# Modulation weights as 64 rows by two column blocks over the partitions: one sum over partitions per vector instead of two

## The reference, cut to what matters

```python
c_silu = jax.nn.silu(c)
mods = jnp.split(c_silu @ ada_w[layer] + ada_b[layer], N_MOD, axis=-1)   # N_MOD = 9, each vector 1024 wide
shift, scale = jnp.split(c_silu @ kv_ada_w + kv_ada_b, 2, axis=-1)
h = modulate(rms_norm(x, norm_g[layer, 0]), sh, sc)                      # h * (1 + sc) + sh
```

## Time and profile before

| what | us |
|---|---|
| median of 3 runs | 1204.28 |
| the runs | 1204.13 to 1204.91 |
| the profiled execution, its own time | 1204.4 |
| span of the profiled execution, first to last instruction | 1202.0 |
| PE busy in it | 1186.9 |
| DVE busy | 799.3 |
| ACT, POOL busy | 586.4, 559.0 |
| DMA, mean | 248 GB/s, 297.92 MB |

### The profile page before, as it was taken

How to read it: one execution, slowest core, us unless ns; L and a number is a source line. 1 busy time by engine, 2 the same in 40 slices (tenths; PEclk the granted TensorE clock), 3 DMA queues, 4 the chain that set the end, 5 groups by cost and what they waited for, 6 DMA issues and landing times.

```text
span 1202.0 us, 15430 instructions
## 1 busy us (share of the span) xinstructions
PE 1186.9 (99%) x5752; PEld 976.4 (81%) x5752; DVE 799.3 (66%) x1118; ACT 586.4 (49%) x764; POOL 559.0 (47%) x417
## 2 busy tenths in 40 slices
PE   9999999999999999999999999999999999999998
PEld 6888788788788888788888888888888887888887
DVE  6885468845786787678768666697673675644423
ACT  5566555665643443454434357444352665544440
POOL 1465334565454443545444226664452463445360
PEclk9999999999999999999999999999999999999999
DMA  9976369845798899459888748798874444766650
GB/s 352 361 272 230 106 237 336 282 161 171 240 349 293 288 352 346 158 169 340 297 309 307 275 176 283 243 332 300 305 296 166 149 156 158 262 218 203 210 192 35
DMA packets 183224, 297.92 MB, mean 248 GB/s; under 512 B 8368, under 2 KB 100208, under 8 KB 183152
## 3 DMA queue, kind: packets, MB, share of 16 engines
q1 hardware_dynamic: 177696, 284.82, 68.0%
q10 hardware_dynamic: 5456, 12.13, 2.9%
HBM read 295.84 MB, written 1.08 MB: 247 GB/s over the span
## 4 chain that ended last, share of the span: by engine, by line
PE 88%; DVE 5%; ACT 2%; issue 1%; SPq 1%; DMA 1%; POOL 1%; ACTq 0%; DVEq 0%
PE ps L1831 26%; PE ps L1844 26%; PE ps L1836 26%; PE ps L2097 2%; PE ps L1981 1%; PE ps L1923 1%; PE ps L1858 1%; PE ps L2009 1%; DVE w_lo L1164 1%; PE ps L1997 1%; DMA raw<-w_in 1%; POOL stat L507 1%; PE ps L1969 1%; PE ps L2020 1%; SPq L474 1%
## 5 line engine op out<-in xcount | busy, mean ns | idle before, releaser
L516 POOL TENSOR_TENSOR w_lo<-raw,w_hi 128x512 fp32r<-128x512 f32 x348 | 480.2, 1411 | 442.5 <-ACT w_hi L647 442.5
L647 ACT ACTIVATE w_hi<-raw 128x2048 fp32r<-128x2048 f32 x188 | 354.5, 1910 | 104.0 <-PE ps L1844 69.3
L1831 PE MATMUL ps<-w_hi,h_hi 128*128 128x512 f32 x1120 | 314.0, 402 | 1.1 <-issue 0.8
L1844 PE MATMUL ps<-w_lo,h_hi 128*128 128x512 f32 x1120 | 301.7, 391 | 1.8 <-DVE w_lo L1164 1.4
L1836 PE MATMUL ps<-w_hi,h_lo 128*128 128x512 f32 x1120 | 300.7, 391 | 0.0
L1164 DVE TENSOR_TENSOR w_lo<-raw,w_hi 128x2048 fp32r<-128x2048 f32 x96 | 223.7, 2334 | 110.8 <-ACT w_hi L647 108.7
L1844 PEld LDWEIGHTS ps<-w_lo,h_hi 128*128 128x128 f32 x1120 | 209.5, 188 | 49.3 <-DVE w_lo L1164 4.0
L1836 PEld LDWEIGHTS ps<-w_hi,h_lo 128*128 128x128 f32 x1120 | 210.4, 188 | 45.9 <-DVE h_lo L1225 0.2
L1831 PEld LDWEIGHTS ps<-w_hi,h_hi 128*128 128x128 f32 x1120 | 200.9, 189 | 43.7 <-issue 6.8
L1150 DVE SCALAR_TENSOR_TENSOR ps<-ada_raw,ccol,ps 128x512 f32<-128x512 f32 x240 | 181.1, 754 | 8.8 <-DMA ada_raw<-ada_w 2.0
L920 ACT ACTIVATE a_hi<-ps 128x512 fp32r<-128x512 f32 x44 | 26.4, 599 | 159.8 <-PE ps L2097 159.8
(11 more groups left out here) (198 smaller groups left out, 978.6 us busy)
## 6 DMA issues: line engine op xcount, KB each, us to landing
raw<-ffn_in SPq DMA_DIRECT2D x176, 512.0 KB, 5.7
ada_raw<-ada_w SPq DMA_DIRECT2D x144, 512.0 KB, 7.2
raw<-ffn_out SPq DMA_DIRECT2D x44, 1024.0 KB, 6.6
raw<-w_in SPq DMA_DIRECT2D x31, 1024.0 KB, 8.8
raw<-w_out SPq DMA_DIRECT2D x8, 1024.0 KB, 5.7
ada_raw<-kv_ada_w SPq DMA_DIRECT2D x16, 512.0 KB, 8.6
raw<-w_kv SPq DMA_DIRECT2D x8, 1024.0 KB, 5.6
bias<-na_bias ACTq DMA_DIRECT2D x16, 256.0 KB, 4.5
```

The lines of the kernel that those rows point to most:

```text
L516: ins = pool.tensor_tensor(w_lo[:, u % RAW, piece], raw[:, u % RAW, piece], w_hi[:, u % RING, piece].bitcast(F32), ALU.subtract)
L647: act.activation(w_hi[:, u % RING, :], raw[:, u % RAW, :], ACT.Copy).then_inc(*S.inc("w_hi_ready", u))
L1831: pe.matmul(bank(b), hi[:, k_in_lhs + k, tok], wh[:, k, c * 512:(c + 1) * 512], start=start and k == 0, stop=False)
L1844: ins = pe.matmul(bank(b), hi[:, k_in_lhs + k, tok], wl[:, k, c * 512:(c + 1) * 512], start=False, stop=stop and k == nk - 1)
```

## The change

The slots hold another cut of the same weights. The partitions are now two blocks of 64: partition p of block k holds a weight row of half k of the columns. A slot is 2 x 64 rows by both halves (1024 columns), so a vector takes 8 slots in one chain of 16 multiply-adds, and one set of four transposes and one reduction for all of it. The layout of silu(c) (`ccol`, 16 columns of 64 rows, twice over the partitions) follows. A slot is now loaded by two DMAs, one for each 64 partitions. `ada_after` is the same table of 160 slots.

```diff
 ADA_RING = 4
+ADA_BLOCKS = 2
-SUM_STEPS = (5, 7, 9, 11, 12, 14, 15, 18, 22, 31)
+SUM_STEPS = (5, 7, 9, 11, 12, 14, 15, 18, 31)
-    HALF_SLOTS = KC // 2
-    N_ADA = N_VEC * 2 * HALF_SLOTS
+    ADA_ROWS, ADA_SET = P // ADA_BLOCKS, ADA_BLOCKS // 2
+    SLOTS, N_SETS = D // (2 * ADA_ROWS), N_VEC // ADA_SET
+    N_ADA = N_SETS * SLOTS
...
-                    rows = w[2 * pair * P:(2 * pair + 2) * P, col:col + 512].rearrange("(k p) n -> p k n", p=P)
-                    sp.dma_start(ada_raw[:, j % ADA_RING], rows).then_inc(ada_in[j % ADA_RING], 16)
+                    for k in range(ADA_BLOCKS):
+                        w, col = vec_src[ADA_SET * g + k // 2]
+                        col += 512 * (k % 2)
+                        rows = w[2 * slot * ADA_ROWS:(2 * slot + 2) * ADA_ROWS, col:col + 512]
+                        sp.dma_start(ada_raw[k * ADA_ROWS:(k + 1) * ADA_ROWS, j % ADA_RING],
+                                     rows.rearrange("(i p) n -> p i n", p=ADA_ROWS)).then_inc(ada_in[j % ADA_RING], 16)
...
-            def reduce_vector(v, half):
-                dve.wait_ge(*S.at("ada_sumT_done", v, half))
-                b = job_bank["ada", v, half]
-                dve.tensor_reduce(mods[:, v, 4 * half:4 * half + 4], bank(b).rearrange("p (k c) -> p k c", k=4),
-                                  AX.X, ALU.add).then_inc(*S.inc("ada_reduced", v, half))
-                if half == 0:
-                    return
+            def reduce_set(g):
+                dve.wait_ge(*S.at("ada_sumT_done", g))
+                blocks = bank(job_bank["ada", g]).rearrange("p (k b r) -> p b k r", k=4, b=ADA_BLOCKS)
+                vectors = range(ADA_SET * g, ADA_SET * g + ADA_SET)
+                m = mods[:, ADA_SET * g:ADA_SET * g + ADA_SET, :].rearrange("p v (h k) -> p (v h) k", h=2)
+                dve.tensor_reduce(m, blocks, AX.X, ALU.add).then_inc(*S.inc("ada_reduced", g))
...
-                for half in sum_step.get((layer, 31), []):
-                    reduce_vector(*half)
+                lows(o + 3)
+                for g in sum_step.get((layer, 31), []):
+                    reduce_set(g)
                 fill(o + 3)
...
-            def ada_sum(v, half):
-
-                pe.wait_ge(*S.at("ada_used", (2 * v + half) * HALF_SLOTS + HALF_SLOTS - 1))
-                b = job("ada", (v, half), ("ada_reduced", v, half))
+            def ada_sum(g):
+
+                pe.wait_ge(*S.at("ada_used", g * SLOTS + SLOTS - 1))
+                b = job("ada", (g,), ("ada_reduced", g))
...
-        "c_cols": cols(get("c_2")[0]),
+        "c_cols": np.tile(get("c_2")[0].reshape(-1, P // ADA_BLOCKS).T, (ADA_BLOCKS, 1)),
```

More of the change, by code:

```diff
@@ L235, in program @@
             taken.add((layer, s))
-            sum_step[layer, s] = [(v, half)]
+            sum_step[layer, s] = [g]
             continue
@@ L240, in program @@
                 e = first[b] + wait + (wait > 1 and first[b] + wait in sum_unit.values())
-        sum_unit[v, half] = e
-    in_pool = max(h for h in sum_unit if sum_unit[h] < first["pool"])
+        sum_unit[g] = e
+    in_pool = max(g for g in sum_unit if sum_unit[g] < first["pool"])
     sum_unit[in_pool] = first["pool"]
-    for h in range(2, len(HALVES)):
-        if HALVES[h - 2] in sum_unit:
-            assert sum_unit[HALVES[h - 2]] + 2 < half_end(*HALVES[h]), HALVES[h]
+    for g in range(2, N_SETS):
+        if g - 2 in sum_unit:
+            assert sum_unit[g - 2] + 2 < set_loaded(g), g
     def up_sum(e):
@@ L255, in up_sum @@
         return None
-    vec_end = [sum_unit.get((v, 1), 0) + 4 for v in range(N_VEC)]
+    vec_end = [sum_unit.get(v // ADA_SET, 0) + 4 for v in range(N_VEC)]
     with ExitStack() as ctx:
@@ L399, in short_work @@
         def short_work(layer, s):
-            work = [("ada_reduce", half) for half in sum_step.get((layer, s - 1), [])]
+            work = [("ada_reduce", g) for g in sum_step.get((layer, s - 1), [])]
             work += [("diff", h) for h in range(HEADS_DA) if DA_DIFF[h] == s]
@@ L410, in short_work @@
             work += [("da_scores", h) for h in range(HEADS_DA) if DA_SCORES[h] == s]
-            work += [("ada", half) for half in sum_step.get((layer, s), [])]
+            work += [("ada", g) for g in sum_step.get((layer, s), [])]
             return work
@@ L1182, in sums @@
                     u = sums_done[0]
-                    for v, half in HALVES:
-                        e = sum_unit.get((v, half), NU)
+                    for g in range(N_SETS):
+                        e = sum_unit.get(g, NU)
                         if e + 4 == u and up_sum(e) is None and e != first["pool"]:
-                            reduce_vector(v, half)
+                            reduce_set(g)
                     for j in ada_at(u):
@@ L1526, in reduce_sums @@
                 def reduce_sums(s):
-                    for v, half in HALVES:
-                        if up_sum(sum_unit.get((v, half), NU)) == (name, s):
-                            reduce_vector(v, half)
+                    for g in range(N_SETS):
+                        if up_sum(sum_unit.get(g, NU)) == (name, s):
+                            reduce_set(g)
                 for s in range(4 * NG):
```

66 lines of the change are left out of this document (34 added, 32 removed).

## The result

The changed kernel takes 1325.47 us at the median against 1204.28: ratio 1.1002, 95% interval 1.0987 to 1.1017. Of its four runs one, 1349.06, ran in a slower state; the median of the other three is 1325.25. I had forecast 1194.0 in a range to 1204. The forecast was wrong in its sign, and the time lies far above rival 1 as well (1228).

A forecast was written before the change was run, and what follows sets the result against it. PE, busy 1186.9 of 1202.0 us, was taken as the bound; 9.2 us (sums) plus 1.5 (w_lo) off, slower loads costing nothing, gave 1193.6, stated as 1194, with a range from 1191.5 to 1204.

The forecast's parts named there:

- rival 1: Slot loads: half-height loads take the full double (f = 2), both FFN stages lose 17 us, 1228 us; chance 0.13 for slower.
- f: Factor on the slots' load time from half-height loads: taken between 1.2 and 1.5, costing nothing below 1.63 in first FFN.
- my sum: Whole run: 9.2 + 1.5 = 10.7 us off the profiled span, 1202.0 to 1191.3, so 1193.6 expected of the runs.
- 21 us of free queue: Window 320 to 465: loads take 124 us of 145 by bytes over rates, leaving 21 us to absorb slower slots.
- The cover: Tightest place, ffn_out raw loads: w_lo ready 8.8 us ahead of PE; with the queue's free time, 30 us of cover.
- Sums: 20 sets of four transposes leave PE between half steps, 0.46 us each: 9.2 us gained, low bound 7.0.
- w_lo: Ends of both encoder layers: two w_lo made ahead of the reduction gain 1.04 and 0.35 to 0.5, 1.5 us in all.
- In the pooling stage the reduction: Pooling stage: bias and finish now follow the reduction, some 0.4 us, hidden by DVE's 0.78 us idle for ACT.
- the reduction, bias and finish now come behind, about 1.1 us: Encoder layers' ends: these follow w_lo while DVE waits for PE's product; costs nothing, by 0.4 us of cover.
- DVE, the reduction's form: DVE: summing eight rows of 64 instead of four of 128 takes 0.69 us, at worst twice that, off the path.
- SP: SP issues 160 DMAs more, 0.47 us each, 75 us within its 766 us of waiting for PE: costs nothing.
- the signs of rival 1: Slots landing well over 10 us, FFN DMA share near 1 at fewer GB/s, PE waiting for weights in the ffn_out product.

The follow-up runs named there:

- split_rows: Kernel before with each slot's load issued as two of 256 KB, each to all 128 partitions, cut by columns; 1203.9 us, ratio 1.000.
- interleaved: Changed kernel with the two blocks on alternate partitions (row r of block k on partition 2r + k, not 64k + r); 1199.81 us, ratio 0.9964.
- Interleaved_gap: The kernel interleaved plus an unused tile of 32 bytes per partition behind ccol; 1193.14 us, ratio 0.9907.

## Why the prediction was wrong, point by point

- **Loads, the step that failed.** "I take a factor f between 1.2 and 1.5, since the two halves of many slots are queued together ..., so that one can write one half while another writes the other." No row stood behind that sentence. It was an argument, and it served to set aside the one source that had measured such a load. As my sum uses it (all that the queue loses, put down to the slots' bytes, with the other loads as fast as before) f came out at 2.1 to 2.25. Two things are in that number. A slot's own packets take 1.59 times as long, just over my range and near the 1.67 that I had worked out by the Trainium skill ("SBUF — State Buffer", the section on the port swizzle) from two single transfers of 1 MiB; on the slots' own packets the trace agrees with that page. The rest is the slowing of the loads beside them, 99 of the 263 us, a term that stood in no sum of mine, with either f.
- **The price of a given f, the second failure.** Rival 1 had f = 2 and came to 1228. Its 21 us of free queue came from bytes over rates, with SP's queue alone. The engines' share in that window is 0.93, ACT's queue included, which leaves 10 us:

```profile
320.00:465.00 145.00, 145.00 (x679) 119.57 (x679) 115.44 (x137) 62.18 (x52) 69.30 (x50) 1.00 0.93 328
```

With 10 in place of 21 my own formula, 47.4 (f - 1) less 19, gives 33 to 41 us a stage for f of 2.1 to 2.25. The first FFN lost 41 and the second 35. And I priced these two stages only: the encoder lost 25 (PE is busy 17.60 of 20 us from 60 on already) and the third FFN 17. Half the slots cut showed that a mean factor of 1.55, which I had called free, costs 51 us in all. In the very rows that I showed, the share is 1.03 for 30 us: there nothing was free, whatever the mean over the stage.
- **The cover.** I priced only raw loads, with ACT's lead of 8.8 us. That DVE waits for slots in program order, ahead of the gates, stood in no step, though the diff shows the wait and the trace of before the 2.0 us. It is the larger way to PE (45.8 us at L2105).
- **The clock** was no term of mine: some 35 of the 123.5 us, by the estimate above.
- **Sums**: 9.2 predicted, 9.0 measured. **w_lo**: 1.5 predicted, 1.8 measured by the spans of the profiled runs, 1.1 by the medians.
- **"In the pooling stage the reduction ... is now followed by bias and finish, some 0.4 us ... which hides it"**: 1.8 us, because POOL was running, and PE paid 1.0. At the second layer's end I had written that "the reduction, bias and finish now come behind, about 1.1 us", for both layers in one sentence, with the cover counted in the first alone. In the second bias and finish are new; 1.0 us.
- **DVE, the reduction's form**: 687 ns a piece, as taken. **SP**: 160 issues more cost nothing, neither in split_rows (0.43 us each) nor in interleaved (0.61 each, where I took 0.47).
- **Not in any step**: 32 bytes in the size of a tile, 4 us.
- Interleaved_gap's 1193.14 beside my 1193.6 is no proof of the sum: 2 us of cost that I missed and 2 us of gain from the better place of `a_hi` cancel.
- **What would show it**: of the signs of rival 1, the landing (11.4 us at the median for `ada_w`), the share near 1 at fewer GB/s came true; PE's waits came at the transposes of the gates rather than in the product with `ffn_out`.

## What to carry to other kernels

Ask of every transfer which partitions it writes, not only how many bytes: here packets to 64 adjacent partitions took 1.59 times as long and slowed their neighbours in the queue, while the same 64 as every second one cost nothing, so a layout in blocks can often be kept by interleaving the blocks. When a cost has no row in the trace, the source that has measured it sets the value, and one's own argument only the bound; and a slower load is to be priced with all that shares its queue. Free time of a queue is to be counted stretch by stretch, against the engine that waits for it first, which may be the one that does side work in program order.

## What the runs showed of the hardware

- Transfers to 32 adjacent partitions are as fast per byte as to 64 adjacent ones; transfers to every fourth or every second partition run within about 2% of the rate of whole ones, in packet time (q1 69.5% and 68.6% of spans of 1202.1 and 1197.7, against 81.8% and 81.6% of 1310.2 and 1321.1).
- With slots going to 64 adjacent partitions, the packets of untouched loads in the same queue take longer too: 65.2 ns for 50.0 (`ffn_in`), 261.2 for 169.7 (`ffn_out`).
- To issue one load of a slot takes SP 0.47 us at the median for 512 KB to 128 partitions, 0.43 for 256 KB to 128 (split_rows) and 0.61 for 256 KB to 64, adjacent or every second one.
- In this kernel matmuls of 512 columns start 2% further apart when the tile that holds their weights starts 32 bytes later (2.80 us for 2.74), and 1% closer at 64 bytes (2.72; `a_hi`, `a_lo`). With `h_hi` and `h_lo` 32 bytes later as well, the kernel took 18 us more.
- A DVE instruction of 8 columns takes 0.17 us by itself and up to 1.22 us while POOL runs a piece of w_lo, ending with it. The Trainium skill has the reason in "SBUF — State Buffer", section "Who interferes with whom": DVE and POOL share a pair of ports, held for a whole instruction. The trace agrees as far as it goes, in all these places.
